# Opening of a hybrid DeltaNet and attention layer: modulation loads cut by features, and their products placed pair by pair

## What is computed

```python
m = jax.nn.silu(cond) @ w_ada + b_ada            # cond: c and c_ctx, two rows
shift1, scale1, gate1, shift2, scale2, gate2 = split(m, 6)
h = rmsnorm(x, norm1_g) * (1 + scale1) + shift1
u = h @ w_in        # q, k, v of 8 heads, z, beta and decay logits, attention q/k/v, gates
# DeltaNet branch: short convolution + SiLU on q, k, v, then a chunked scan per head
# neighbourhood attention branch, gated merge, w_out, then a SwiGLU feed-forward block
```

## Time and profile before

| | us |
|---|---|
| median of 3 runs | 1408.74 |
| lowest, highest | 1407.41, 1413.54 |
| the profiled execution | 1407.62 |
| its span in the profile | 1405.8 |
| TensorE busy in the span | 1358.4 |

### The profile page before, as it was taken

One profiled execution on the slowest core, in us unless ns is written; L12 is line 12 of the kernel. 1 busy time (PEld: TensorE's weight loads), 2 busy tenths in 40 slices (PEclk: granted clock), 3 DMA queues, 4 the chain that ended last, 5 costly groups with the idle time before them and its releaser, 6 DMA issues.

```text
span 1405.8 us, 26274 instructions
## 1 busy us (share of the span) xinstructions
PE 1358.4 (97%) x10442; PEld 1270.0 (90%) x10442; DVE 814.2 (58%) x1739; ACT 672.3 (48%) x1480; POOL 224.0 (16%) x189
## 2 busy tenths in 40 slices
PE   5999999999999999999999998999999999999998
PEld 4888989899998989999897877999999999999998
DVE  6466655756565565656535654757866434666422
ACT  4463736455373645537346554436655212555321
POOL 1020020202002020200030322000344002444100
PEclk8999999999999999999999999999999999999999
DMA  9552533142333324213426223522232322332332
GB/s 312 201 139 75 153 95 111 55 132 74 89 107 95 111 56 140 66 59 113 130 70 218 68 69 117 169 76 61 60 91 61 103 73 68 103 90 62 83 90 68
DMA packets 202560, 144.49 MB, mean 103 GB/s; under 512 B 8719, under 2 KB 188215, under 8 KB 202183
## 3 DMA queue, kind: packets, MB, share of 16 engines
q1 hardware_dynamic: 202439, 142.82, 34.3%
HBM read 126.77 MB, written 17.99 MB: 103 GB/s over the span
## 4 chain that ended last, share of the span: by engine, by line
PE 75%; DVE 12%; ACT 6%; issue 3%; SPq 2%; DMA 2%; POOL 0%; DVEq 0%; ACTq 0%
PE ps L1199 23%; PE ps L1728 16%; PE ps L1765 11%; PE ps L1498 7%; PE ps L1425 2%; PE ps L1369 1%; DVE tri L2613 1%; PE ps L1432 1%; PE ps L1273 1%; PE ps L1444 1%; DVE tri L2654 1%; DMA W<-in_w_in 1%; DVE W_r L2607 1%; PE ps L1443 1%; PE ps L1375 1%
## 5 line engine op out<-in xcount | busy, mean ns | idle before, releaser
L1199 PE MATMUL ps<-hT_r,WAH_r 128*128 128x320 f32 x912 | 228.4, 331 | 5.6 <-ACT zs L2061 2.4
L1199 PE MATMUL ps<-xT_r,WAH_r 128*128 128x320 f32 x912 | 207.4, 308 | 0.0
L1199 PEld LDWEIGHTS ps<-hT_r,WAH_r 128*128 128x128 f32 x912 | 145.0, 189 | 24.8 <-issue 11.5
L1199 PEld LDWEIGHTS ps<-xT_r,WAH_r 128*128 128x128 f32 x912 | 152.6, 188 | 0.0
L1199 PE MATMUL ps<-hT_r,W_r 128*128 128x320 f32 x592 | 133.9, 309 | 0.0
L1765 PE MATMUL ps<-a_part,W_r 128*128 128x320 f32 x704 | 132.3, 310 | 0.0
L3155 POOL TENSOR_TENSOR gm<-sqkq,dt 128x1280 f32<-128x1280 f32 x8 | 23.5, 2938 | 572.8 <-DVE Xc L2649 502.5
L1765 PEld LDWEIGHTS ps<-a_part,W_r 128*128 128x128 f32 x704 | 110.3, 188 | 0.0
L1728 PE MATMUL ps<-t_big_r,W_r 128*128 128x320 f32 x380 | 107.2, 310 | 0.6 <-ACT naT L2316 0.5
L1728 PE MATMUL ps<-b_part,W_r 128*128 128x320 f32 x456 | 101.4, 309 | 1.4 <-DVE oT_r L2925 1.4
L1199 PEld LDWEIGHTS ps<-hT_r,W_r 128*128 128x128 f32 x592 | 99.1, 189 | 0.0
(11 more groups left out here) (436 smaller groups left out, 3258.9 us busy)
## 6 DMA issues: line engine op xcount, KB each, us to landing
oT<-in_ffn_w SPq DMA_DIRECT2D x44, 512.0 KB, 5.2
W<-in_w_in SPq DMA_DIRECT2D x36, 512.0 KB, 4.0
WAH<-in_w_ada SPq DMA_DIRECT2D x18, 1024.0 KB, 6.8
naT<-in_w_in SPq DMA_DIRECT2D x24, 512.0 KB, 4.2
oT<-in_ffn_w SPq DMA_DIRECT2D x16, 704.0 KB, 4.6
ext_dram<-naT SPq DMA_DIRECT2D x28, 320.0 KB, 4.1
GCB<-gc_dram SPq DMA_DIRECT2D x7, 640.0 KB, 4.2
W<-in_w_pa SPq DMA_DIRECT2D x8, 512.0 KB, 3.7
```

The costliest lines, as they stand in the source:

```text
L1199: m = e.matmul(ps[:, bank + b, 0:n], w[:, k, :], x[:, k, a:a + n], start=k == 0 and i == 0, stop=k == KD - 1 and i == 2, skip_group_check= ...
```

## The change

- A modulation group now belongs to two blocks: group n holds 256 columns of shift and 256 columns of scale for blocks 2n and 2n + 1. Its two DMAs are the shift half and the scale half, each with all eight k. They carry 1 MB as before, in pieces of 1 KB where there were 2 KB.
- TensorE does a group as 8 products of 256 columns for each half (16 in all, shift first). Group 0 and its turn stand alone; groups 1, 2 and 3 stand in front of strip block q 0, q 2 and q 4, and their turns behind that block. All turns use one bank (`TURNED`), so a turn waits for VectorE's sum of the one before.
- The stream of TensorE is then regular: group, q block, turn, q block, two logits blocks, two k blocks.
- `gains` is called four times, for two blocks each. VectorE's normalisation of blocks 4 to 7 is spread between them. The remainder of strip v and the masks come after the last block.
- `wba` has a semaphore of its own (`ld_wba`) and is loaded between group 1 and strip k. Strip q is loaded between group 0 and group 1. The eight other small loads come behind strip k.
- GpSimd's three memsets wait for the last block of h as well.

The diff, cut to its core:

```diff
-        ADA_ORDER, ADA_BANK = (0, 2, 1, 3), (6, 7, 7, 6)
+        WP_OF, ROW_BANK, TURNED = (0, 2, 1, 3), (1, 6, 6, 6), 7
+        QW = 2 * P
...
-            def ada_in(i):
-                for j in range(2):
-                    e.dma_start(WP[i][:, 4 * j:4 * j + 4, :], w_ada[:, 4 * j:4 * j + 4, i * 4 * P:(i + 1) * 4 * P]).then_inc(ld_wp[i][j], 16)
+            def ada_in(n):
+                i = WP_OF[n]
+                for s in range(2):
+                    e.dma_start(WP[i][:, :, s * QW:(s + 1) * QW], w_ada[:, :, s * D + n * QW:s * D + (n + 1) * QW]).then_inc(ld_wp[i][s], 16)
...
             ada_in(0)
-            ada_in(2)
             opening_in("q")
+            ada_in(1)
+            e.dma_start(wba[:, :, :], w_in[:, :, OFF_BETA:OFF_BETA + 4 * H]).then_inc(ld_wba, 16)
             opening_in("k")
...
-            e.dma_start(wba[:, :, :], w_in[:, :, OFF_BETA:OFF_BETA + 4 * H]).then_inc(ld_ba, 16)
...
-            ada_in(1)
+            ada_in(2)
             ada_in(3)
...
             def ada_group(n):
...
+                if n >= 2:
+                    e.wait_ge(ada_row, n)
+                for s in range(2):
+                    e.wait_ge(ld_wp[i][s], 16)
+                    for k in range(KD):
+                        j = k % 4
+                        m = e.matmul(ps[32 * j:32 * j + 32, bank, s * QW:(s + 1) * QW], csT[:, k, :], WP[i][:, k, s * QW:(s + 1) * QW],
+                                     start=k < 4, stop=k >= 4, skip_group_check=True)
+                m.then_inc(ada_mm, 1)
 
             def ada_select(n):
                 e.wait_ge(ada_row, n + 1)
+                if n:
+                    e.wait_ge(ada_out, 2 * n - 1)
...
             ada_group(0)
-            ada_group(1)
             ada_select(0)
-            ada_select(1)
...
+            for n in range(4):
+                if n < 3:
+                    ada_group(n + 1)
+                e.wait_ge(h_done, 2 * n + 1)
+                opening_mm("q", 2 * n)
+                if n < 3:
+                    ada_select(n + 1)
+                e.wait_ge(h_done, 2 * n + 2)
+                opening_mm("q", 2 * n + 1)
+                for k in (2 * n, 2 * n + 1):
+                    logits_mm(k)
+                for k in (2 * n, 2 * n + 1):
+                    opening_mm("k", k)
...
             ada_out_row(0)
-            ada_out_row(1)
             opening_big(OPENING_BIG["q"], W[:, slot["q"], :, :], ld_w["q"], 16)
             round_h(0)
-            opening_big(wbas[:, :, 0, :], wba[:, :, :], ld_ba, 16 * 9)
             round_h(1)
+            ada_out_row(1)
+            opening_big(wbas[:, :, 0, :], wba[:, :, :], ld_wba, 16)
...
+            for k in range(4):
+                normed(k)
             e.wait_ge(vec_out, 1)
             gains(0)
             exact_h(0)
+            exact_h(1)
             opening_kind("q", 1)
             small_h(0)
-            exact_h(1)
+            small_h(1)
             opening_small(wbas[:, :, 1, :], wba[:, :, :], wbas[:, :, 0, :], 2)
-            small_h(1)
+            normed(4)
+            gains(1)
             opening_kind("k", 3)
             exact_h(2)
             exact_h(3)
             small_h(2)
             small_h(3)
-            e.wait_ge(ld_ba, 16 * 9)
+            normed(5)
+            gains(2)
+            exact_h(4)
+            normed(6)
+            exact_h(5)
+            small_h(4)
+            small_h(5)
+            normed(7)
+            gains(3)
+            exact_h(6)
+            small_h(6)
+            exact_h(7)
+            small_h(7)
+            e.wait_ge(ld_ba, 16 * 8)
             e.tensor_scalar(msk[:, :, :], sq_c[:, LE:GE + 1, :], 1.0, -NEG, ALU.subtract, ALU.mult).then_inc(zero_done, 1)
-            opening_kind("v", 4)
...
+            opening_kind("v", 4)
...
             e.wait_ge(ada_mm, 2)
+            e.wait_ge(h_done, KD)
             e.memset(LNTd[:, :, :], 0.0)
```

More of the change, by code:

```diff
@@ L431, in build @@
         ld_ba = sem("ld_ba")
+        ld_wba = sem("ld_wba")
         ba_mm = sem("ba_mm")
@@ L1841, in _ @@
             ada_out_row(0)
-            ada_out_row(1)
             opening_big(OPENING_BIG["q"], W[:, slot["q"], :, :], ld_w["q"], 16)
             round_h(0)
-            opening_big(wbas[:, :, 0, :], wba[:, :, :], ld_ba, 16 * 9)
             round_h(1)
+            ada_out_row(1)
+            opening_big(wbas[:, :, 0, :], wba[:, :, :], ld_wba, 16)
             opening_big(OPENING_BIG["k"], W[:, slot["k"], :, :], ld_w["k"], 16)
+            round_h(2)
+            round_h(3)
+            ada_out_row(2)
+            e.wait_ge(ld_ba, 16 * 8)
             e.activation(alog[:, :], alog[:, :], ACT.Exp).then_inc(ba_act, 1)
-            for k in range(2, KD // 2):
-                round_h(k)
-            ada_out_row(2)
+            round_h(4)
+            round_h(5)
             ada_out_row(3)
             opening_big(OPENING_BIG["v"], W[:, slot["v"], :, :], ld_w["v"], 16)
-            for k in range(KD // 2, KD):
-                round_h(k)
+            round_h(6)
+            round_h(7)
             e.wait_ge(zero_done, 3)
@@ L2437, in _, with normed, gains @@
             e.wait_ge(x_out, 2 * NT)
-            for k in range(KD):
+            def normed(k):
                 e.tensor_tensor(xn[:, k, :], xs[:, k, :], rstd[:, :], ALU.mult).then_inc(xn_done, 1)
-            def gains(half):
-                a, z = 4 * half, 4 * half + 4
+            def gains(n):
+                a, z = 2 * n, 2 * n + 2
                 both_rows = mods[:, 0:16, :].rearrange("p (s k) c -> p s k c", s=2)[:, :, a:z, :]
-                b = cols[:, B_ADA:B_ADA + 16].rearrange("p (s k) -> p s k", s=2)[:, :, a:z].unsqueeze(3).to_broadcast([P, 2, 4, 2])
+                b = cols[:, B_ADA:B_ADA + 16].rearrange("p (s k) -> p s k", s=2)[:, :, a:z].unsqueeze(3).to_broadcast([P, 2, 2, 2])
+                e.wait_ge(ada_sel, n + 1)
+                parts = ps[:, TURNED, :].rearrange("p (s k g r) -> p s k r g", s=2, k=2, g=4)
                 for j in range(2):
-                    n = 2 * half + j
-                    e.wait_ge(ada_sel, n + 1)
-                    parts = ps[:, ADA_BANK[n], :].rearrange("p (k g r) -> p k r g", k=4, g=4)[:, :, 0:2, :]
-                    m = e.tensor_reduce(both_rows[:, j, :, :], parts, AX.X, ALU.add)
+                    m = e.tensor_reduce(both_rows[:, j, :, :], parts[:, j, :, 0:2, :], AX.X, ALU.add)
                 m.then_inc(ada_out, 1)
-                e.wait_ge(ada_out, 2 * half + 1)
+                e.wait_ge(ada_out, 2 * n + 1)
                 e.tensor_tensor(both_rows, both_rows, b, ALU.add).then_inc(ada_out, 1)
-                e.wait_ge(ada_out, 2 * half + 2)
-                e.scalar_tensor_tensor(gain1[:, a:z, :], mods[:, 8 + a:8 + z, :], 1.0, cols[:, N1 + a:N1 + z].unsqueeze(2).to_broadcast([P, 4, 2]), ALU.add, ALU.mult).then_inc(gain_done, 1)
-                e.wait_ge(gain_done, half + 1)
+                e.wait_ge(ada_out, 2 * n + 2)
+                e.scalar_tensor_tensor(gain1[:, a:z, :], mods[:, 8 + a:8 + z, :], 1.0, cols[:, N1 + a:N1 + z].unsqueeze(2).to_broadcast([P, 2, 2]), ALU.add, ALU.mult).then_inc(gain_done, 1)
+                e.wait_ge(gain_done, n + 1)
             def exact_h(k):
@@ L2482, in _ @@
             small_h(3)
-            e.wait_ge(ld_ba, 16 * 9)
+            normed(5)
[11 more added lines that the diff above has]
+            small_h(7)
+            e.wait_ge(ld_ba, 16 * 8)
             e.tensor_scalar(msk[:, :, :], sq_c[:, LE:GE + 1, :], 1.0, -NEG, ALU.subtract, ALU.mult).then_inc(zero_done, 1)
-            opening_kind("v", 4)
-            gains(1)
             e.memset(raws[:, :, 0:1], 0.0)
@@ L2489, in _ @@
             e.memset(raws[:, :, 2 + TOK:4 + TOK], 0.0).then_inc(zero_done, 1)
-            exact_h(4)
-            for k in range(KD // 2, KD):
-                if k < KD - 1:
-                    exact_h(k + 1)
-                small_h(k)
+            opening_kind("v", 4)
             def taps_of(h):
```

25 lines of the change are left out of this document (4 added, 21 removed).

## The result

| | before | changed |
|---|---|---|
| median, us | 1408.97 (20 runs) | 1412.03 (20 runs) |
| lowest, highest | 1406.48, 1413.54 | 1409.78, 1415.97 |
| changed over before | | 1.0020, 95% interval 1.0012 to 1.0028 |
| profiled execution, its span | 1407.62, 1405.8 | 1411.02, 1409.2 |

Two repetitions gave 1.0017 (1.0005 to 1.0029) and 1.0022 (1.0010 to 1.0033). The changed kernel is 2.3 to 3.1 us slower by the medians. The forecast was no change, 1408.2 in a range that ends at 1411.8, and it was wrong: the median lies just outside, and all three intervals lie above 1. The loss is small beside the 0.5% that the forecast called measurable, but 20 runs of each kernel tell it from nothing.

What follows compares the result with a forecast made beforehand. TensorE, busy 1358.4 of 1405.8 us, bounds the kernel. 1.6 us gained by order and 1.6 lost by the clock sum to 0.0; between 1407.6 and 1408.7 it took 1408.2, range 1404.2 to 1411.8.

Steps and rivals of the forecast that it cites:

- behind it the opening's work is the same in both kernels: From strip v's start, 58.9 us before, TensorE is the bound; a shift there should reach the end almost whole.
- Behind the opening: Rival: head 0's loads meet the store of x and the memsets otherwise; up to 3 us either way, chance 0.08.
- The forecast's own test: Steps are wrong if strip v starts on time and the end still moves by more than 1 us, among other signs.
- The third group is issued at 27.65.: SyncE passes the squares' load at 23.65, then issues the third modulation group 4.0 us later; 27.33 before, bounds 25.85 to 28.65.
- T = 37.1: Moment in the opening when the third modulation group's load is complete, in us; bounds 35.3 to 38.1.
- the break-even of 38.7: Completion time of the third group's load, in us, past which the change becomes a loss; 37.1 with the clock's fall.
- No wait for the fourth group: In the opening, TensorE takes the fourth modulation group, loaded at about 42.5 us, without waiting.
- The clock falls in the new gap: TensorE idles 3.1 us before the third group's second half, then runs at 1.2 GHz, losing 1.6 us; rival clock holds, 0.27.
- The fall at 751 us: Attention part, kernel before: half clock from 751.5 to 754.5 after 1.5 us idle from 748.1, used as precedent.
- Small pieces: Rival: modulation groups' 1 KB pieces load at 298 GB/s, not 382; 4.7 us slower, 1412.9, chance 0.09.
- +1.6 and -1.6 in the opening: 1.6 us gained by the new order, strip v at 57.3 against 58.9, and 1.6 lost by TensorE's clock falling.
- the forecast's two cases: Strip v's first product at 57.3 us if the clock holds, or at 58.9 if it falls.

Runs made afterwards that it cites:

- the repetition: The changed kernel as it is, run and profiled a second time: median 1412.30 us, 1.0017 over before.
- with SyncE free: Changed kernel with the eight small loads issued behind strip v's load and ScalarE's exponential behind the last block of h: 1407.08 us, 0.9991 over before.

## Why the prediction was wrong, step by step

- *"behind it the opening's work is the same in both kernels and TensorE is the bound, so a shift of it should reach the end almost whole."* This step failed. The sum put the stretch behind the opening at nothing. The shift did reach 838 us whole (-0.72 at 62 us, -0.86 at 800). But the stretch behind the opening was not the same in one respect, the place of TensorE's instruction fetches in it, and 4.3 us went there in the trace; with the fetches moved back by 64 products the kernel gained 3.7 us in the mean. The rival "Behind the opening" had a chance of 0.08 and a bound of 3 us, but named the wrong cause, the loads of head 0 and the memsets. The forecast's own test, strip v on time and the end moved by more than 1 us, is what came.
- *"The third group is issued at 27.65."* Wrong: 30.35, later than every bound given. The assumed moment at which SyncE passes the squares' load failed: 25.74 where I had 23.65 (21.85 before), since strip k's own issue in front of it ended only at 22.7. Behind it 4.6 us lie up to the group, not 4.0: `alog` took 0.43 as assumed, the four gain columns 3.1.
- *T = 37.1, range 35.3 to 38.1.* 38.9, outside. By the break-even of 38.7 the opening should have been 0.2 us longer. It was 0.7 shorter, since the work behind T was over-priced by 0.9 us, mainly in the turns: a turn is four transposes and took 0.60 us, and I had put the 1.04 that eight took the earlier trace rows, twice.
- *No wait for the fourth group, 0.9 us idle before q 7, memsets and strip v's remainder hidden.* Right: 45.27 without a wait, 0.88 us, GpSimd's memsets from 54.3 us without an effect on TensorE.
- *The clock falls in the new gap, 1.6 us.* Right as a mechanism and a matter of chance in each execution: at full in the first trace, at half for 6.8 us in the repetition, where it cost 2.3 us. The fall at 751 us that I set beside it stands behind idle time in which VectorE worked on the operands of the next product (the chain of before, `oT_r` and `hT` from 748.10 us on), and not behind a wait for a load.
- *Small pieces.* Not the cause: with SyncE free the third group was there by 33.6 us, and the opening 4.9 us shorter.
- The forecast time, 1408.2, was made of +1.6 and -1.6 in the opening. What the two first traces show in its place: opening 0.7 gained (1.6 gained to 1.6 lost in the changed kernel's three traces), table 1.8 lost, clock behind it 1.5 lost, 0.8 lost at 880. That the opening itself came out between the forecast's two cases is luck in part: a load later by 1.8 us and turns priced too high nearly cancelled.

**Open.** The 0.6 to 0.9 us at 880, where VectorE waits for `tB`: 3.6 to 3.9 us in the three traces of before, 4.3 to 5.5 in all others. Eight of these have a fetch between the issue of `tB` and its use and wait 4.3 to 5.5 us; three have none there and wait 4.3 to 4.6 all the same, so the fetch is not all of it. That the fetch packet takes one of the DMA engines which the table's load needs fits the single packet in flight at the load's end, but the trace doesn't name the engines. How much of the 3 us the late table and what follows it cost in a typical execution, and how much other moved fetches do, isn't separated. Why the clock falls near 76 us with some shorter openings and not with others was not tried.

## What to carry to other kernels

When a change of the opening loses time far behind it, align the two traces and look at the first step in the offsets before thinking about the opening; then compare everything that moved in that window, the instruction fetches of the DMA view too. Adding instructions to a long stream moves all later fetches, and a load with no slack can win or lose by it, so an edit should be judged once more with its instruction count padded by half a fetch, here 64 matmuls and their weight loads. And closing a wait in front of the engine that bounds the kernel (small loads behind the groups, 4.2 us of the opening) was worth more than the reordering around it (0.7 us).

## What the runs showed of the hardware

- TensorE's instructions arrive by DMA during the execution, in packets of 16 KB, one for 255 to 256 instructions; a packet takes 0.9 to 2.1 us. 64 matmuls more, half a packet, turned a load of 3.1 us into one of 4.6 us in before and one of 5.1 into 3.1 in the changed kernel. The Trainium skill (Trainium Architecture — The Big Picture, The software stack) tells only that the instruction streams are brought to the engines when the program is loaded; the traces show fetches all through the run, 83 or 84 for TensorE.
- A load with such a packet in it ends late on one engine's share alone: in the changed kernel one packet at a time was in flight over its last 0.8 us, where about 16 are in its middle.
- Moving the fetches by half a packet cost or gained more than the delay of the one load: 1.3 to 1.9 us of delay, 3.6 to 3.7 us in the mean of the runs. In 7 of 7 traces with the late table the granted clock fell to half between 846 and 859 us, in 1 of 7 without.
- Three traces of one kernel, before, end 3 us apart (-0.5 to +2.5), mainly by two stretches at half clock, at 856 and 883 us. One trace of either kernel could not have told this change.
